# Hybrid decoder trunk on one core: unit norms on column and row tiles, and the delta scan's keys times state first

## Chip, cores and metric

One core of a Trainium2 chip runs the whole kernel. The metric is the time of one execution on the device in microseconds; 0.2% of it is 3.7 us.

## What is computed

Two layers of a decoder trunk, sequence 512, width 1024, all in f32. Each layer joins three token mixers (sparse attention A, gated delta rule B, retention C) by gates, projects, and adds a squared-ReLU MLP of width 4096. The change touches branch B, which has four heads of width 128:

```python
qb = l2_norm(qb.reshape(bsz, seq, B_HEADS, B_HEAD_DIM))   # x * rsqrt(sum(x*x) + EPS)
kb = l2_norm(kb.reshape(bsz, seq, B_HEADS, B_HEAD_DIM))
...
t_inv = solve_triangular(eye + m, eye)                    # m: strict lower part of k_beta @ k^T * decay
u = t_inv @ (v * beta);  w = t_inv @ (k_beta * exp(g))
# scan over chunks
v_new = u - w @ state
o = (q * exp(g)) @ state + a_intra @ v_new
state = state * exp(g_last) + (k * exp(g_last - g))^T @ v_new
```

## The kernel before

Weights stream from memory in slabs of 128x1024. GpSimd (or ScalarE) rounds a slab to a high part, VectorE subtracts to get the low part (L1094), and TensorE makes three products per tile (L1229 to L1231: high-high, high-low, low-high), 24 matmuls of 512 columns a slab. Raw, high and low parts have two buffers, so the low part of slab n + 2 is made after slab n has been used. Dense results go round four banks psD; the small matmuls go round three banks psM[0] to psM[2], with psM[3] for accumulations. small_bank (in the TensorE program) waits until the step that last had the bank has been read; `drained` names that reader, bank_plan (L612) gives the banks in TensorE's order.

The order is written in one list for all engines. Its prefix is by hand (L165 to L190): misc, twelve convolution slabs (keys, queries, values of the four heads) with SiLU, va, four rotation slabs, the first cv slab. `every` (L529) expands it: for each step its TensorE, ScalarE and VectorE part; a slab's low part for two slabs later (`lo`) comes on VectorE right behind the VectorE part of that slab's step. In the prefix the eight unit norms are spread over four rounds, two per round. One norm is unit_sq on ScalarE (squares to sqs, two buffers, L1764), a 128x128 matmul with ones (`unit`, L1362), which gives each of the 128 partitions the sum over the partitions, Ln and Exp on ScalarE into gt (L1772, L1774), and a product on VectorE (L2199). The first round is followed by `rows`, a transpose (L1395) of the decay columns.

The middle is planned by a list scheduler in the same file with a cost per step and a rank by the longest path behind it; it mixes the delta scan, retention, attention and slabs in four pieces. Each chunk n of 128 positions has four heads. In the scan vn, kk, kq and kn are turns and products of the chunk (L1294, L1288); then the 16x16 blocks are solved through memory and merged in levels (left, xx, xt; L1429, L1441, L1453). After them:

```python
# n >= 1, before
Kp = K[n] * (beta * exp(g))            # VectorE L2307, K[n] is kn's turned copy
wT = Kp^T X                            # TensorE L1288, ScalarE copies it times -1 to P1 (L1858)
v2 = X^T v + P1^T St                   # TensorE L1476, L1479, ScalarE copies (L1861)
oT = ...                               # TensorE L1489, L1492
St = St * exp(g_last) + K''^T v2       # VectorE L2324 (Sd), TensorE st L1288, VectorE L2331 (St)
```

where X is the inverse and K'' is K times kps (Kpp, L2319). A hand-written tail (the last gate and merge slabs, the output projection) and the MLP follow.

Of the kernel before, what the change touches and what calls it, by code (L numbers as in the profile page):

```python
# [23 lines left out]
ALU = mybir.AluOpType  # L24
# [3 lines left out]
P = 128  # L28
# [44 lines left out]
PIECES = 4  # L73

# [29 lines left out]
for _name, _w in (("ident", P), ("ones", P), ("cosA", S), ("sinA", S), ("cosI", S), ("sinI", S), ("cosR", S), ("sinR", S), ("decay", H * S),  # L104
                  ("tri", P), ("maskadd", P), ("cap", P),
                  ("level", (LEVELS - 1 - FIRST) * P)):
# [12 lines left out]
def tables():  # L119
# [32 lines left out]
    put("level", np.concatenate(lv, 1))  # L152
    return t
# [5 lines left out]
def schedule():  # L159
# [7 lines left out]
    for j in range(CONVS):  # L167
# [3 lines left out]
        if j >= 1:  # L171
            prefix.append(("silu", j - 1))
    prefix += [("va",), ("silu", CONVS - 1), ("unit_sq", 0), ("unit_sq", 1), ("decays",), ("rot", 0), ("va_turn",),
               ("gcum",)]
    for r in range(4):
# [4 lines left out]
        for j in (2 * r, 2 * r + 1):  # L180
            prefix.append(("unit", j))
            if j + 2 < 2 * H:
                prefix.append(("unit_sq", j + 2))
# [40 lines left out]
    for n in range(ST):  # L224
        for i, (x, t) in enumerate((("vn", .44), ("kk", .9), ("kq", .9), ("kn", .44))):
            drains = {"vn": ("dve", "vb", n), "kk": ("dve", "MT", n), "kq": ("dve", "AT", n), "kn": ("act", "K", n)}
            op("pe", x, n, t=t, to=drains[x], after=[("dve", "AT", n - 1)] + [("dve", "decay", n)] * (i > 0))
# [4 lines left out]
        op("act", "K", n, t=copied(), after=[("pe", "kn", n), ("act", "E", n)])  # L232
# [8 lines left out]
    for n in range(ST):  # L241
# [287 lines left out]
    def every(steps, n, ahead=()):  # L529
# [3 lines left out]
        for s in steps:  # L533
# [78 lines left out]
def bank_plan():  # L612
# [14 lines left out]
    for s in PE_ORDER:  # L627
# [7 lines left out]
        elif k in ("unit", "va_turn", "misc_turn", "fin", "gcum", "rows"):  # L635
# [52 lines left out]
def build(nc, ws, wo, wd, par, post, tab, x_in, out, rows_d, mt_d, x_d, xt_d):  # L688
    with ExitStack() as ctx:
# [45 lines left out]
        with ExitStack() as mix:  # L735
# [1981 lines left out]
```

## Time and profile before

| what | us |
|---|---|
| median of 3 runs (lowest, highest) | 1860.92 (1860.22, 1861.11) |
| the profiled execution | 1859.46 |
| its span, first to last instruction | 1857.6 |
| TensorE busy | 1830.2 |
| VectorE busy | 1247.8 |
| ScalarE busy | 750.9 |
| GpSimd busy | 265.4 |

The granted clock of TensorE was 0.998 of its full rate. Matmuls are pipelined: their busy times overlap, so the time that one occupies is read from the distance of two starts. An f32 matmul leaves two records; an fp32r matmul and an f32 transpose leave one. A layer takes about half of the span; the second layer's steps lie some 922 us after the first's.

### The profile page before, as it was taken

To read this page: it belongs to the slowest core of one execution; us is meant where nothing else is said; L and a number is where in the kernel's file an instruction comes from. 1 tells how busy PE (TensorE), PEld (TensorE's weight loads), DVE (VectorE), ACT (ScalarE), POOL (GpSimd) and SP (SyncE) were. 2 spreads that over 40 slices of the span, in tenths; PEclk is the share of its full clock that TensorE was granted. 3 is DMA by queue.
4 is the path that set the end of the run, shared out by engine and by line. 5 is a ranking of instruction groups with operands and counts; after the bars stand their busy time and mean duration, and the time that the engine had idled before them with its cause. 6 is when DMAs were issued, how large, how long until landed. Compare 5 with 4: busy or idle time off the path is not lost.

```text
span 1857.6 us, 23921 instructions
## 1 busy us (share of the span) xinstructions
PE 1830.2 (99%) x8878; PEld 1467.8 (79%) x8878; DVE 1247.8 (67%) x2072; ACT 750.9 (40%) x1261; POOL 265.4 (14%) x385
## 2 busy tenths in 40 slices
PE   8999999999999999999999999999999999999997
PEld 6877767788888888888778777677887888888886
DVE  6856789854475667575878658898534657575748
ACT  3163343322334635454531533533123346354454
POOL 2221111111120010000012211111112201100000
PEclk9999999999999999999999999999999999999999
DMA  6432113322441794766522322223225308856654
GB/s 239 146 126 85 62 63 98 88 80 69 145 150 46 210 255 138 202 181 170 166 100 93 125 74 69 69 89 97 80 69 190 138 13 249 226 150 191 194 135 102
DMA packets 87041, 240.22 MB, mean 129 GB/s; under 512 B 19920, under 2 KB 32400, under 8 KB 85904
## 3 DMA queue, kind: packets, MB, share of 16 engines
q1 hardware_dynamic: 46656, 171.76, 26.7%
q0 software_dynamic: 10368, 37.75, 10.9%
q10 hardware_dynamic: 29904, 29.19, 4.8%
q8 instruction: 72, 1.18, 0.3%
q14 instruction: 41, 0.34, 0.1%
HBM read 227.62 MB, written 11.06 MB: 128 GB/s over the span
## 4 chain that ended last, share of the span: by engine, by line
PE 90%; DVE 4%; ACT 3%; issue 2%; DMA 1%; DVEq 0%; POOL 0%; ACTq 0%; SPq 0%
PE psD L1229 24%; PE psD L1231 23%; PE psD L1230 23%; PE psM L1229 3%; PE psM L1230 3%; PE psM L1231 3%; PE psM L1288 1%; PE psM L1294 1%; PE psM L1507 1%; PE psM L1386 1%; PE psM L1525 1%; PE psM L1513 1%; PE psM L1378 1%; ACT wide L1757 1%; DVE wide L2536 1%
## 5 line engine op out<-in xcount | busy, mean ns | idle before, releaser
L1229 PE MATMUL psD<-a_hi,w_hi 128*128 128x512 f32 (+2 forms) x1488 | 595.3, 400 | 0.9 <-DVE w_lo L1094 0.6
L1231 PE MATMUL psD<-a_hi,w_lo 128*128 128x512 f32 (+2 forms) x1488 | 575.1, 386 | 0.0
L1230 PE MATMUL psD<-a_lo,w_hi 128*128 128x512 f32 (+2 forms) x1488 | 574.2, 386 | 0.0
L1094 DVE TENSOR_TENSOR w_lo<-raw,w_hi 128x1024 fp32r<-128x1024 f32 x216 | 263.5, 1221 | 142.6 <-POOL w_hi L1196 98.0
L1229 PEld LDWEIGHTS psD<-a_hi,w_hi 128*128 128x128 f32 (+1 forms) x1488 | 278.9, 187 | 79.3 <-issue 21.6
L1231 PEld LDWEIGHTS psD<-a_hi,w_lo 128*128 128x128 f32 (+1 forms) x1488 | 278.8, 187 | 57.8
L1230 PEld LDWEIGHTS psD<-a_lo,w_hi 128*128 128x128 f32 (+1 forms) x1488 | 279.2, 188 | 56.7 <-issue 4.8
L2524 DVE TENSOR_TENSOR d_lo<-d_raw,d_hi 128x1024 fp32r<-128x1024 f32 x102 | 124.1, 1222 | 69.2 <-ACT d_hi L2054 69.2
L1196 POOL TENSOR_SCALAR w_hi<-raw 128x1023 fp32r<-128x1023 f32 x150 | 166.2, 1108 | 0.0
L1195 POOL TENSOR_TENSOR w_hi<-raw,tabs 128x1 fp32r<-128x1 f32 x150 | 34.9, 233 | 896.3 <-PE psD L1231 865.3
L1203 POOL DMA_DIRECT2D d_raw<-in_wd x72 | 63.3, 961 | 642.8 <-DMA d_raw<-in_wd 437.7
L2054 ACT CAST d_hi<-d_raw 128x1024 fp32r<-128x1024 f32 x102 | 105.9, 1046 | 104.2 <-PE psM L1231 41.2
L2040 ACT CAST w_hi<-raw 128x1024 fp32r<-128x1024 f32 x62 | 65.1, 1049 | 84.8 <-PE psD L1231 84.3
L1229 PE MATMUL psM<-d_hi,f_hi 128*128 128x512 f32 x240 | 94.3, 393 | 0.1
L1230 PE MATMUL psM<-d_lo,f_hi 128*128 128x512 f32 x240 | 93.4, 389 | 0.0
L1231 PE MATMUL psM<-d_hi,f_lo 128*128 128x512 f32 x240 | 93.4, 389 | 0.0
L1757 ACT COPY wide<-psD 32x512 f32<-32x512 f32 (+1 forms) x84 | 48.7, 579 | 78.9 <-DVE iq L2184 34.5
L1229 PE MATMUL psD<-y_hi,w_hi 128*128 128x512 f32 x192 | 77.4, 403 | 0.0
L1231 PE MATMUL psD<-y_hi,w_lo 128*128 128x512 f32 x192 | 74.8, 390 | 0.0
L1230 PE MATMUL psD<-y_lo,w_hi 128*128 128x512 f32 x192 | 74.8, 390 | 0.0
L2048 ACT CAST f_hi<-gt 128x768 fp32r<-128x768 f32 x64 | 60.6, 947 | 29.3 <-DVE gt L2512 28.2
L2518 DVE TENSOR_TENSOR f_lo<-gt,f_hi 128x768 fp32r<-128x768 f32 x64 | 69.8, 1091 | 3.6
(301 smaller groups left out, 2786.5 us busy)
## 6 DMA issues: line engine op xcount, KB each, us to landing
raw<-in_ws SPq DMA_DIRECT2D x216, 512.0 KB, 3.5
d_raw<-in_wd SPq DMA_DIRECT2D x88, 512.0 KB, 5.9
d_raw<-in_wd POOLq DMA_DIRECT2D x72, 512.0 KB, 8.4
s_raw<-in_wo ACTq DMA_DIRECT2D x14, 512.0 KB, 11.5
tabs<-in_tab SPq DMA_DIRECT2D x2, 2880.0 KB, 12.0
x<-rows_d ACTq DMA_DIRECT2D x4, 1024.0 KB, 5.7
x<-out ACTq DMA_DIRECT2D x2, 2048.0 KB, 8.4
x<-in_x SPq DMA_DIRECT2D x4, 512.0 KB, 5.4
```

The costliest lines, as they stand in the source:

```text
L1094: dve.tensor_tensor(w_lo[:, s, :], raw[:, s, :], w_hi[:, s, :].bitcast(F32), ALU.subtract) \
L1196: pool.tensor_scalar(w_hi[:, s, 1:], raw[:, s, 1:], 1.0, 1.0, ALU.mult, ALU.mult) \
L1203: pool.dma_start(home(name), down_slab(c, b, j), accum_op=ALU.add).then_inc(*inc("sum_" + name[:None if name[0] == "C" else 1], 16))
L1229: pe.matmul(out, lhi, rhi, start=start, stop=False, skip_group_check=more)
L1230: pe.matmul(out, lhi, rlo, start=False, stop=False, skip_group_check=more)
L1231: return pe.matmul(out, llo, rhi, start=False, stop=stop, skip_group_check=more)
L1757: sig(act.copy(wt[to:to + n, 6 + r % 2, :], src[at:at + n, :]), "rot_copy" if to + n == P else "rot_part")
L2040: act.copy(w_hi[:, s, :], raw[:, s, :]).then_inc(sem("w_hi"), 1)
L2048: sig(act.copy(f_hi[:, p, w, :], fr[:, w, :]), "f_hi" + part)
L2054: sig(act.copy(operand(c, st)[0], source(st)), "d_hi")
L2518: sig(dve.tensor_tensor(f_lo[:, p, w, :], fr[:, w, :], f32(f_hi[:, p, w, :]), ALU.subtract), "f_lo" + part)
L2524: sig(dve.tensor_tensor(lo, source(st), f32(hi), ALU.subtract), "d_lo")
```

## The change

- The squares of four heads lie in one buffer, sq4, and each is made with the last four convolutions (keys) or behind the first sum (queries). sq4 lies where cv comes later.
- `usum` g makes four matmuls of 128 rows and 32 columns of ones, head h into partitions 32h to 32h + 31 of one bank. ScalarE takes Ln and Exp once for all four.
- `spread` g makes four matmuls of 32 rows with a table that is one in each first row of a quarter, each into a bank of its own (three of the small ones and psM[3]). VectorE multiplies straight with the banks.
- In the prefix: usum 0 ahead of rotation 0; spread 0, usum 1 and spread 1 behind rotations 1, 2 and 3.
- The scan multiplies keys by state first (`ks`), VectorE scales the product and subtracts it from v (`ku`, two products), and v2 is one matmul a head. Kp, wT and its copy go. The keys of chunk n are turned only behind ks; the last chunk's not at all.
- The table `first` adds 128 columns.

```diff
@@ -103,7 +104,7 @@
 _at = 0
 for _name, _w in (("ident", P), ("ones", P), ("cosA", S), ("sinA", S), ("cosI", S), ("sinI", S), ("cosR", S), ("sinR", S), ("decay", H * S),
                   ("tri", P), ("maskadd", P), ("cap", P),
-                  ("level", (LEVELS - 1 - FIRST) * P)):
+                  ("level", (LEVELS - 1 - FIRST) * P), ("first", P)):
     TAB[_name] = (_at, _w)
     _at += _w
 NTAB = _at
...
@@ -150,6 +151,7 @@
         a, b = row[:, None] >> l, row[None, :] >> l
         lv.append((b == a + 1) & (b % 2 == 1))
     put("level", np.concatenate(lv, 1))
+    put("first", np.repeat(row[:, None] % QUARTER == 0, P, 1))
     return t
 
 
...
@@ -170,17 +172,17 @@
             prefix.append(("misc_turn",))
         if j >= 1:
             prefix.append(("silu", j - 1))
-    prefix += [("va",), ("silu", CONVS - 1), ("unit_sq", 0), ("unit_sq", 1), ("decays",), ("rot", 0), ("va_turn",),
-               ("gcum",)]
+        if j >= CONVS - H:
+            prefix.append(("unit_sq", j - (CONVS - H)))
+    prefix += [("va",), ("silu", CONVS - 1), ("decays",), ("usum", 0)] + [("unit_sq", H + h) for h in range(H)]
+    prefix += [("rot", 0), ("va_turn",), ("gcum",)]
     for r in range(4):
         if r < 3:
             prefix.append(("rot", r + 1))
         else:
             prefix += [("piece", j, "cv", 0) for j in range(PIECES - 1)] + [("cv", 0)]
-        for j in (2 * r, 2 * r + 1):
-            prefix.append(("unit", j))
-            if j + 2 < 2 * H:
-                prefix.append(("unit_sq", j + 2))
+        if r < 3:
+            prefix.append((("spread", 0), ("usum", 1), ("spread", 1))[r])
         if r == 3:
             prefix.append(("rot", 4))
         prefix.append(("turn", r))
...
@@ -223,13 +225,16 @@
         op("dve", "decay", n, t=4 * read(1, slow), after=[("act", "decay", n)])
     for n in range(ST):
         for i, (x, t) in enumerate((("vn", .44), ("kk", .9), ("kq", .9), ("kn", .44))):
+            if x == "kn" and n:
+                continue
             drains = {"vn": ("dve", "vb", n), "kk": ("dve", "MT", n), "kq": ("dve", "AT", n), "kn": ("act", "K", n)}
             op("pe", x, n, t=t, to=drains[x], after=[("dve", "AT", n - 1)] + [("dve", "decay", n)] * (i > 0))
         op("act", "E", n, t=copied(), after=[("dve", "decay", n)])
         op("dve", "vb", n, t=read(4, 1.1), after=[("pe", "vn", n)])
         op("dve", "MT", n, t=read(4, slow) + read(), after=[("act", "E", n), ("pe", "kk", n), ("dve", "vb", n)])
         op("dve", "AT", n, t=read() + read(4, slow), after=[("pe", "kq", n), ("dve", "MT", n), ("act", "decay", n)])
-        op("act", "K", n, t=copied(), after=[("pe", "kn", n), ("act", "E", n)])
+        if n == 0:
+            op("act", "K", n, t=copied(), after=[("pe", "kn", n), ("act", "E", n)])
         if n + 2 < ST:
             op("act", "decay", n + 2, t=copied(), after=[("dve", "AT", n)])
             op("dve", "decay", n + 2, t=4 * read(1, slow), after=[("act", "decay", n + 2), ("dve", "decay", n + 1)])
...
@@ -260,16 +265,16 @@
             else:
                 op("pe", "xt", n, l, t=.55, to=("dve", "XT", n, l), after=[("act", "left", n, l), ("act", "XT", n, l - 1)])
                 op("dve", "XT", n, l, t=read(2, 1.2), after=[("pe", "xt", n, l)])
-        over = [("pe", "wT", n - 1)] if n >= 2 else []
         if n:
-            op("dve", "Kp", n, t=read(4, slow), after=[("act", "K", n), ("dve", "Kpp", n - 1)] + over)
+            op("pe", "ks", n, t=.9, to=("dve", "ku", n), after=[("dve", "St", n - 1), ("dve", "AT", ST - 1)])
+            op("dve", "ku", n, t=read(4, 1.1) + read(4, slow), after=[("pe", "ks", n), ("dve", "vb", n), ("dve", "Kpp", n - 1)])
+            if n < ST - 1:
+                op("pe", "kn", n, t=.44, to=("act", "K", n), after=[("pe", "ks", n)])
+                op("act", "K", n, t=copied(), after=[("pe", "kn", n)])
         if n < ST - 1:
-            op("dve", "Kpp", n, t=read(4, slow), after=[("act", "K", n), ("dve", "Kp", n), ("dve", "AT", ST - 1)])
-        if n:
-            op("pe", "wT", n, t=.9, to=("act", "wT", n), after=[("dve", "XT", n, LEVELS - 1), ("dve", "Kp", n)])
-            op("act", "wT", n, t=copied(), after=[("pe", "wT", n)])
-        op("pe", "v2", n, t=1.8 if n else .9, to=("act", "v2", n),
-           after=[("dve", "XT", n, LEVELS - 1), ("dve", "vb", n), ("act", "wT", n), ("dve", "St", n - 1)])
+            op("dve", "Kpp", n, t=read(4, slow), after=[("act", "K", n), ("dve", "AT", ST - 1)])
+        op("pe", "v2", n, t=.9, to=("act", "v2", n),
+           after=[("dve", "XT", n, LEVELS - 1), ("dve", "vb", n)] + [("dve", "ku", n)] * (n > 0))
         op("act", "v2", n, t=copied(), after=[("pe", "v2", n)])
         op("pe", "oT", n, t=1.8 if n else .9, to=("act", "oT", n), after=[("act", "v2", n), ("dve", "AT", n), ("dve", "St", n - 1)])
         op("act", "oT", n, t=copied(), after=[("pe", "oT", n)])
...
@@ -539,7 +544,7 @@
             if s[0] in STREAMED and s != ("rot", 4):
                 late.append(("dve", "lo", n + 2))
                 n += 1
-            if s[0] not in ("va", "silu", "unit_sq", "decays"):
+            if s[0] not in ("va", "silu", "unit_sq", "usum", "decays"):
                 o += late
                 late = []
         return o
...
@@ -632,7 +637,10 @@
                 [("p1" if k == "left" else "ro" if k == "rv" else k, *(s[1:2] if k == "rv" else s[1:]))]
             for name, b in zip(names, TAKEN[s]):
                 use(name, b)
-        elif k in ("unit", "va_turn", "misc_turn", "fin", "gcum", "rows"):
+        elif k == "spread":
+            for h in range(H):
+                use((*s, h), 3 if h == H - 1 else None)
+        elif k in ("usum", "va_turn", "misc_turn", "fin", "gcum", "rows"):
             use(s)
         elif k in ("rv", "av") and s[2] == 0:
             use(("ro" if k == "rv" else "ao", s[1]), 3)
...
@@ -747,6 +755,9 @@
                 cv = sb("cv", [P, ST, S], where=u)
                 rp = sb("rp", [P, 2, S], where=u)
             with ExitStack() as u:
+                sb("cqk_place", [P, 4, S], where=u)
+                sq4 = sb("sq4", [P, H, S], where=u)
+            with ExitStack() as u:
                 sc = sb("sc", [P, S], where=u)
                 work = sb("work", [P, S], where=u)
                 rl = sb("rl", [P, 2, S], where=u)
...
@@ -1035,8 +1051,8 @@
                 return [(f"X{a[0] % 2}", 2 * inner_count(*a))]
             if k == "xt":
                 return [(f"XT{a[0] % 2}", level_count(*a))]
-            if k == "wT":
-                return [("wTn", a[0])]
+            if k == "ks":
+                return [("Ku", 2 * a[0] - 1)]
             if k == "v2":
                 return [("vnew", a[0] + 1)]
             if k == "oT":
...
@@ -1354,12 +1370,20 @@
                         if r != 4:
                             dense_T(("rot", r))
 
-                    def unit(j):
-                        if j == 0:
-                            pe.wait_ge(kept["tables_in"], 16 * (layer + 1))
-                        pe.wait_ge(*on("unit_sq", j + 1))
-                        ps = small_bank(("unit", j))
-                        small_done(pe.matmul(ps[:, :], T("ones"), sqs[:, j % 2, :], start=True, stop=True))
+                    def usum(g):
+                        pe.wait_ge(*on("unit_sq", H * g + H))
+                        ps = small_bank(("usum", g))
+                        for h in range(H):
+                            ins = pe.matmul(ps[quad(h), :], T("ones")[:, 0:QUARTER], sq4[:, h, :], start=True, stop=True)
+                        small_done(ins)
+
+                    def spread(g):
+                        pe.wait_ge(kept["tables_in"], 16 * (layer + 1))
+                        pe.wait_ge(*on("unit_r", g + 1))
+                        spots = [small_bank(("spread", g, h)) for h in range(H)]
+                        for h in range(H):
+                            small_done(pe.matmul(spots[h][:, :], T("first")[quad(h), :], gt[quad(h), 2 + g, :],
+                                                 start=True, stop=True))
 
                     def cv_tiles(i, ts):
                         u = DENSE["cv", 0]
...
@@ -1459,26 +1483,17 @@
                                 pe.wait_ge(*on(s, v))
                             turn_heads(("xt", n, l), lambda h: B["X", n % 2][:, cut(h)])
 
-                    def scan_w(n):
-                        pe.wait_ge(*on(f"XT{n % 2}", level_count(n, LEVELS - 1)))
-                        pe.wait_ge(*on("Kp", n))
-                        by_heads(("wT", n), lambda h: B["Kp"][:, cut(h)], lambda h: B["XT", n % 2][:, cut(h)])
+                    def scan_k(n):
+                        pe.wait_ge(*on("St", n))
+                        by_heads(("ks", n), lambda h: kB(h, n), lambda h: B["St"][:, cut(h)])
 
                     def scan_v(n):
 
                         pe.wait_ge(*on(f"XT{n % 2}", level_count(n, LEVELS - 1)))
                         pe.wait_ge(*on("vb", n + 1))
                         if n:
-                            pe.wait_ge(*on("wTn", n))
-                            pe.wait_ge(*on("St", n))
-                        ps = small_bank(("v2", n))
-                        for h in range(H):
-                            ins = pe.matmul(ps[:, cut(h)], B["XT", n % 2][:, cut(h)], qkv[:, 2 * H + h, cut(n)],
-                                            start=True, stop=n == 0)
-                            if n:
-                                ins = pe.matmul(ps[:, cut(h)], B["P1", n % 2][:, cut(h)], B["St"][:, cut(h)],
-                                                start=False, stop=True)
-                        small_done(ins)
+                            pe.wait_ge(*on("Ku", 2 * n))
+                        by_heads(("v2", n), lambda h: B["XT", n % 2][:, cut(h)], lambda h: qkv[:, 2 * H + h, cut(n)])
 
                     def scan_o(n):
                         pe.wait_ge(*on("vnew", n + 1))
...
@@ -1758,21 +1773,18 @@
                                 "rot_copy" if to + n == P else "rot_part")
 
                     def unit_sq(j):
-                        if j >= 2:
-                            mid(act, ("unit", j - 2))
+                        if j >= H:
+                            mid(act, ("usum", 0))
                         act.wait_ge(*on("silu", j + 1))
-                        sig(act.activation(sqs[:, j % 2, :], qkv[:, j, :], ACT.Square), "unit_sq")
-
-                    def unit(j):
-                        ps = mid(act, ("unit", j))
-                        if j >= 2:
-                            act.wait_ge(*on("unit_done", j - 1))
-                        rt = gt[:, 2 + j % 2, :]
-
+                        sig(act.activation(sq4[:, j % H, :], qkv[:, j, :], ACT.Square), "unit_sq")
+
+                    def usum(g):
+                        ps = mid(act, ("usum", g))
+                        rt = gt[:, 2 + g, :]
                         sig(act.activation(rt, ps[:, :], ACT.Ln, bias=4 * EPS), "unit_ln")
                         own("unit_ln")
                         sig(act.activation(rt, rt, ACT.Exp, scale=-0.5,
-                                           bias=0.0 if j < H else float(-0.5 * np.log(P))), "unit_r")
+                                           bias=float(-0.5 * np.log(P)) if g else 0.0), "unit_r")
 
                     def cv_(i):
                         if i < 3:
...
@@ -1853,9 +1865,6 @@
 
                     def turned(n, l):
                         sig(act.copy(B["XT", n % 2], mid(act, ("xt", n, l))[:, :]), f"XT{n % 2}")
-
-                    def scan_w(n):
-                        sig(act.mul(B["P1", n % 2], mid(act, ("wT", n))[:, :], -1.0), "wTn")
 
                     def scan_v(n):
                         sig(act.copy(MT[n], mid(act, ("v2", n))[:, :]), "vnew")
...
@@ -2194,9 +2203,10 @@
                         own("rot_sin")
                         sig(dve.tensor_tensor(dst, dst, other, ALU.add), "rot_done")
 
-                    def unit(j):
-                        dve.wait_ge(*on("unit_r", j + 1))
-                        sig(dve.tensor_tensor(qkv[:, j, :], qkv[:, j, :], gt[:, 2 + j % 2, :], ALU.mult), "unit_done")
+                    def spread(g):
+                        for h in range(H):
+                            qk = qkv[:, H * g + h, :]
+                            sig(dve.tensor_tensor(qk, qk, mid(dve, ("spread", g, h))[:, :], ALU.mult), "unit_done")
 
                     def rp_(h, m):
                         i, w = RET[h, m], S - m * P
...
@@ -2298,14 +2308,16 @@
                         sig(dve.tensor_tensor(odd, odd, ps[0:HALF, 0:H * HALF].rearrange("p (h c) -> p h c", h=H),
                                               ALU.subtract), f"XT{i}")
 
-                    def kp_(n):
-                        if n == 1:
+                    def ku(n):
+                        v, t = qkv[:, 2 * H:, cut(n)], heads(B["Ku"])
+                        ps = mid(dve, ("ks", n))
+                        if n > 1:
+                            own("Ku")
+                        else:
                             own("bk")
-                        else:
-                            mid(dve, ("wT", n - 1))
-                        dve.wait_ge(*on("K", n + 1))
-                        sig(dve.tensor_tensor(heads(B["Kp"]), qkv[:, 0:H, cut(n)], over(egl[:, n * H:(n + 1) * H], P),
-                                              ALU.mult), "Kp")
+                        sig(dve.tensor_tensor(t, heads(ps[:, :]), over(egl[:, n * H:(n + 1) * H], P), ALU.mult), "Ku")
+                        own("Ku")
+                        sig(dve.tensor_tensor(v, v, t, ALU.subtract), "Ku")
 
                     def kpp(n):
                         k = qkv[:, 0:H, cut(n)]
...
@@ -2313,9 +2325,7 @@
                             dve.wait_ge(*on("esm", 3))
                             own("qs")
                             sig(dve.tensor_tensor(egl, beta, egc, ALU.mult), "bk")
-                            dve.wait_ge(*on("K", 1))
-                        else:
-                            own("Kp")
+                        dve.wait_ge(*on("K", n + 1))
                         sig(dve.tensor_tensor(k, k, over(kps[:, n * H:(n + 1) * H], P), ALU.mult), "Kpp")
 
                     def sd(n):
```

## Rows read from the trace of the kernel before

**Rows 1.** The page: busy time (share) xinstructions; chain that ended last, by engine.
```profile
PE 1830.2 (99%) x8878; PEld 1467.8 (79%) x8878; DVE 1247.8 (67%) x2072; ACT 750.9 (40%) x1261; POOL 265.4 (14%) x385
...
PE 90%; DVE 4%; ACT 3%; issue 2%; DMA 1%; DVEq 0%; POOL 0%; ACTq 0%; SPq 0%
```
**Rows 2.** Waits of TensorE by line: us in total, times, longest.
```profile
PE psM L1085 <- DVE wide L853: 11.1, 2, 7.6
...
PE psM L1362 <- ACT sqs L1764: 1.1, 2, 0.5
```
**Rows 3.** Timeline of TensorE around unit norms: start us, us, engine, line, operation.
```profile
106.84 0.39 PE L1231 MATMUL psD<-a_hi,w_lo 128*128 128x512 f32 x1
107.07 1.88 PE L1362 MATMUL psM<-sqs,tabs 128*128 128x512 f32 x4
108.79 0.27 PE L1395 MATMUL psM<-tabs,small 128*32 128x128 f32 x1
...
109.13 0.40 PE L1230 MATMUL psD<-a_lo,w_hi 128*128 128x512 f32 x1
...
128.60 0.39 PE L1231 MATMUL psD<-w_hi,a_lo 128*128 128x512 f32 x1
...
130.69 1.13 PE L1362 MATMUL psM<-sqs,tabs 128*128 128x512 f32 x2 [0.54 <-ACT sqs L1764]
...
131.89 0.39 PE L1230 MATMUL psD<-w_lo,a_hi 128*128 128x512 f32 x1
```
**Rows 4.** The same timeline behind the slab of va.
```profile
100.51 0.60 PE L1294 MATMUL psM<-tabs,bw 128*128 128x128 f32 x4
100.94 0.29 PE L1344 MATMUL psM<-small,tabs 128*128 128x16 f32 x2
101.55 0.47 PE L1229 MATMUL psD<-a_hi,w_hi 128*128 128x512 f32 x1 [0.31 <-DVE w_lo L1094]
```
**Rows 5.** The same timeline: a pair of 64-row matmuls; sixteen of 64x64.
```profile
168.29 0.39 PE L1231 MATMUL psD<-a_hi,w_lo 128*128 128x512 f32 x1
168.61 1.13 PE L1378 MATMUL psM<-cqk 64*128 64x512 f32 x4
169.67 0.50 PE L1229 MATMUL psD<-a_hi,w_hi 128*128 128x512 f32 x1
170.00 0.39 PE L1230 MATMUL psD<-a_lo,w_hi 128*128 128x512 f32 x1
...
408.54 0.68 PE L1429 MATMUL psM<-x 64*64 64x64 f32 x16
```
**Rows 6.** Timeline of VectorE, then of GpSimd, behind rotation 1.
```profile
107.27 0.69 DVE L2184 TENSOR_TENSOR cqk<-psD,tabs 128x512 f32<-128x512 f32 x1 [3.45 <-PE psD L1231]
108.56 1.23 DVE L1094 TENSOR_TENSOR w_lo<-raw,w_hi 128x1024 fp32r<-128x1024 f32 x1 [0.60 <-POOL w_hi L1196]
...
107.47 1.06 POOL L1196 TENSOR_SCALAR w_hi<-raw 128x1023 fp32r<-128x1023 f32 x1
```
**Rows 7.** Groups of VectorE by shape: busy, mean ns | idle before and its releaser.
```profile
L2199 DVE TENSOR_TENSOR qkv<-qkv,gt 128x512 f32<-128x512 f32 x16 | 11.1, 692 | 20.7 <-ACT gt L1774 20.7
...
L2184 DVE TENSOR_TENSOR cqk<-psD,tabs 128x512 f32<-128x512 f32 x8 | 5.5, 684 | 6.9 <-PE psD L1231 6.9
```
**Rows 8.** Timeline of TensorE: keys times keys between two slabs.
```profile
288.67 1.05 PE L1288 MATMUL psM<-qkv 128*128 128x128 f32 x8
...
289.80 0.40 PE L1230 MATMUL psD<-a_lo,w_hi 128*128 128x512 f32 x1
```
**Rows 9.** Groups of TensorE by shape: v2's second matmul, then the scan's wT.
```profile
L1479 PE MATMUL psM<-bw,x 128*128 128x128 f32 x48 | 9.3, 275 | 0.0
...
L1288 PE MATMUL psM<-x,bw 128*128 128x128 f32 x48 | 6.3, 275 | 0.0
```
**Rows 10.** The same groups from 431.8 to 472.9 us: the slabs there.
```profile
L1229 PE MATMUL psD<-a_hi,w_hi 128*128 128x512 f32 x18 | 7.8, 433 | 0.0
...
L1229 PE MATMUL psD<-y_hi,w_hi 128*128 128x512 f32 x8 | 3.5, 441 | 0.0
```

More of the change, by code:

```diff
@@ L73 @@
 PIECES = 4
+QUARTER = P // 4
 A11, A12, A22, S1, S2, S3, S4, A21 = range(8)
@@ L880, in build @@
         eg = [bw[:, 8 + i, :] for i in range(2)]
-        B = {"misc": bw[:, 8, :], "va": bw[:, 9, :], "rows": bw[0:2 * ST * H, 8, 0:P], "Kp": bw[:, 8, :], "St": bw[:, 9, :]}
+        B = {"misc": bw[:, 8, :], "va": bw[:, 9, :], "rows": bw[0:2 * ST * H, 8, 0:P], "Ku": bw[:, 8, :], "St": bw[:, 9, :]}
         gcr, br_ = [xw[:, n, :] for n in range(ST)], [xw[:, ST + n, :] for n in range(ST)]
@@ L976, in evens, with quad @@
             return ap.rearrange("p (m two b) -> p m two b", two=2, b=2 ** l)[:, :, 0, :]
+        def quad(h):
+            return slice(h * QUARTER, (h + 1) * QUARTER)
         def cut(n):
@@ L1011, in drained @@
                 return [("gc", 1)]
-            if k == "unit":
+            if k == "usum":
                 return [("unit_ln", a[0] + 1)]
+            if k == "spread":
+                return [("unit_done", H * a[0] + a[1] + 1)]
             if k == "misc_turn":
@@ L1554, in _ @@
                              "va": va_, "rot": rot,
-                             "unit": unit, "va_turn": va_turn, "cv": cv_, "rs": rs, "rv": rv, "rows": rows,
-                             "vn": vn, "kk": kk, "kq": kq, "kn": kn, "left": left, "xx": xx, "xt": xt, "wT": scan_w,
+                             "usum": usum, "spread": spread, "va_turn": va_turn, "cv": cv_, "rs": rs, "rv": rv, "rows": rows,
+                             "vn": vn, "kk": kk, "kq": kq, "kn": kn, "left": left, "xx": xx, "xt": xt, "ks": scan_k,
                              "v2": scan_v, "oT": scan_o, "st": st, "index": index, "as": as_,
@@ L1959, in _ @@
                     steps = {"norm": norm, "silu": silu, "decays": decays, "va": va_, "rot": rot,
-                             "unit_sq": unit_sq, "unit": unit, "misc": misc, "va_turn": va_turn, "cv": cv_, "ret": ret,
+                             "unit_sq": unit_sq, "usum": usum, "misc": misc, "va_turn": va_turn, "cv": cv_, "ret": ret,
                              "rows": rows, "rows_in": rows_in, "lasts": lasts, "decay": decay, "E": e_, "K": k_,
                              "mt_out": mt_out, "blk_in": blk_in, "y_out": y_out, "x_in": x_in_, "left": left, "XT": turned,
-                             "wT": scan_w, "v2": scan_v, "oT": scan_o,
+                             "v2": scan_v, "oT": scan_o,
                              "index": index, "sexp": sexp, "prob": prob, "pt": pt_, "attend": attend, "fin_sq": fin_sq, "fin": fin,
@@ L2446, in _ @@
                              "rot": rot, "turn": turn,
-                             "unit": unit, "rp": rp_, "lasts": lasts, "decay": decay, "vb": vb_, "MT": mt_, "AT": at_, "solve": solve,
-                             "lev": lev, "Kp": kp_, "Kpp": kpp, "lvl": lvl, "X": x_, "XT": xt_, "Sd": sd, "St": st_,
+                             "spread": spread, "rp": rp_, "lasts": lasts, "decay": decay, "vb": vb_, "MT": mt_, "AT": at_, "solve": solve,
+                             "lev": lev, "ku": ku, "Kpp": kpp, "lvl": lvl, "X": x_, "XT": xt_, "Sd": sd, "St": st_,
                              "lo": lambda n: lo_slab(dve, n), "index": index, "top": top, "smax": smax, "rinv": recip, "fin": fin,
```

## The prediction

> **What bounds the kernel now.** I read the page first. TensorE is busy 1830.2 of 1857.6 us and carries 90% of the chain that ended last [rows 1]: a change saves time only by what it takes out of TensorE's own row of work, and costs time where TensorE waits in order. Then its waits by line: 11.1 us at the starts of the layers, and 1.1 us before the unit norms; the scan's steps hardly appear [rows 2]. So I priced every TensorE step that is removed or added, and then looked for waits that other engines would now impose. The profiled execution took 1859.46 us, 1.86 more than its span and 1.46 less than the median of the runs; I sum against it and carry the difference over to the median.
>
> Busy times of TensorE overlap, so prices are differences of starts. The split matmul of the slabs has a pitch of 0.227 us (106.84 to 107.07 [rows 3]). The price of a step between slabs is from the last slab start plus 0.227 to the second slab start after it minus 0.227.
>
> **Unit norms, before.** Two norms (four records, as each f32 matmul leaves two) last from 107.07 to 108.79: 0.86 each. With the transpose of the rows behind them the stretch is 109.13 - 0.227 - 107.07 = 1.84, so that transpose costs 0.12. Three rounds of a layer cost 1.72 (one with the 0.12); the fourth goes from 128.60 + 0.227 to 131.89 - 0.227, 2.84, since it waits for squares (0.54 of it just before its second norm) [rows 3]. A layer: 3 x 1.72 + 0.12 + 2.84 = 8.12. Ahead of them, after va's turn (0.43) and gcum, the next slab waits 0.31 for its low part [rows 4].
>
> **Unit norms, after.** Two sums (four matmuls of 32 output partitions) and two spreads (four of 32 contracted partitions). The nearest row is the pair of 64-row matmuls of 512 columns at 168.61: the stretch is 170.00 - 0.227 - 168.29 - 0.227 = 1.26 where two full ones cost 1.72, and a gap of 0.09 precedes the group [rows 5]. So tiles run side by side and what is left is one matmul, 0.86, plus 0.40 of changing over. The 64x64 tiles (sixteen records in 0.68) use other rows and columns [rows 5]; no row has tiles that share their rows and differ in columns, as the sums have. Bounds for a group of four: 1.26 if all run together, 4 x 0.86 + 0.40 = 3.84 if one by one. I take 1.26, from the pair. The same section gives 2.38 times for three column tiles of 512 columns; no row here shows it.
>
> First sum: its squares are issued beside the last four convolutions and are ready when va's slab ends; 1.26. The second sum and the second spread find their inputs done a slab earlier (on ScalarE twelve of sixteen pairs of Ln and Exp go), 1.26 each.
>
> **The first spread brings a wait.** Behind it on TensorE stands the transpose of the rows. Small banks turn over three; after misc_turn, usum, va_turn, gcum and spread (0), the rows get the bank of the first factor of that spread, and must wait until VectorE has multiplied with it (unit_done 1). VectorE has, in its written order, first the rotation's product and the low part of the slab after next. Rotation 1 ends at T = 107.07 [rows 3]: the low part waits for GpSimd's high part (107.47 + 1.06) and runs 108.56 to 109.79, T + 2.7 [rows 6]. A product with a PSUM operand of 128x512 takes 0.68, one in SBUF 0.69 [rows 7]; so the first factor is used at T + 3.3 and TensorE, done with the spread near T + 1.1, stands until T + 3.4. With the transpose and the restart the stretch is 3.6, 2.2 of it new wait. Before, the rows waited only for ScalarE's Ln of an old norm. Behind the rows are queued rotation 2 and all slabs; there is no other TensorE work in the prefix to cover it. Bounds: no wait at all (1.38) if the product came ahead of the low part, 3.6 as written; the order is written, so 3.6.
>
> The decays move ahead of two squares on ScalarE, and an extra 1.26 lies before rotation 0; so the 0.31 wait [rows 4] goes. Layer after: 1.26 + 3.6 + 1.26 + 1.26 - 0.31 = 7.07 against 8.12: **-1.05**, for two layers -2.1.
>
> VectorE's sixteen products stay, with PSUM operands, at one price [rows 7]. The tables grow by 64 KB; no long wait of TensorE names them [rows 2], so nothing.
>
> **Scan, removed and added.** Four heads of 128x128 in eight records cost 289.80 - 0.227 - 288.67 = 0.90 with slabs on both sides and no gap [rows 8]. Per layer: wT three times, -2.70 (48 records in all [rows 9]); the second matmul of v2 three times, -2.70 (48 records); keys times state three times, +2.70; and the turn of the last chunk's keys, -0.43 (a turn has half the records [rows 4]). Sum **-3.1** a layer, -6.2. kn of chunks 1 and 2 only move. On VectorE Kp goes and ku brings two (0.69 each [rows 7]), three times a layer, +2.1; VectorE is not what ends the waits there. ScalarE loses three scalings and one copy.
>
> New chain per chunk: state, ks (0.90), two products of ku (1.38), two hand-offs (0.25 each, an estimate from 107.07 to the VectorE start at 107.27), then v2: 2.8 us. It lies beside slabs: from the first v2 to the end of the scan (431.85 to 473) 26 triples of slab matmuls are interspersed, 26 x 0.68 = 17.7 us [rows 10], against 3 x 2.8 = 8.4, and ks needs no inverse, so it can run while the blocks are inverted, where wT had to follow them. I set 0.25 a layer for steps that fall awkwardly: +0.5.
>
> **Sum.** -2.1 - 6.2 + 0.5 = -7.8: 1851.7 for the profiled execution, **1853.1** for the median.
>
> **Rivals.**
> (1) No wait before the rows. For it: the factor's product is short. Against: the order [rows 6]. Then -4.4 more: 1848.7.
> (2) The four column tiles of a sum don't run together, or only in part. For it: no row has such tiles. Against: pairs overlap fully. Whole: (3.84 - 1.26) x 4 = +10.3, 1863.4; in halves, 1858.3. This is also the case in which the change does not do what it says.
> (3) Slower: the scan's chain becomes the bound at the last chunk's v2. TensorE runs out of slabs between the scan's steps, and the saved matmuls turn into waits. Price: with every link uncovered 2 x 8.4 = 16.8 in place of the -6.2 + 0.5, so 1860.92 - 2.1 + 16.8 = 1875.6. It decides once more than 7.8 us stand uncovered and is slower by more than the measurement tells from 11.5 us. For it: chunk 3's steps end the planned part and behind them the order is fixed. Against: 17.7 us of slabs [rows 10], and the inverse, not the state, releases chunk 3 now.
>
> **How the numbers follow.** Forecast 0.57; rival 1 0.12; rival 2 whole 0.12, in part 0.09; rival 3 0.05; the rest, waits that I don't see, 0.05. About 0.2% (3.7 us) is what can be told from no change: faster means below 1857.2, slower above 1864.6. Faster: 0.57 + 0.12 + a third of the partial case + some of the rest, 0.74. Slower: rival 3 and part of the rest, 0.06. Same 0.20. The range leaves out rival 3 and the ends of the others: 1848.2 to 1862.8; the bottom is rival 1, the top near the whole of rival 2. The likeliest case alone spans 1851 to 1856.
>
> **What would show it.** Right: the sums and spreads as groups of eight records that last some 1.1 us each; one wait of about 2.2 us per layer before the transpose of the rows, released by VectorE's product; no wait for squares in the norms; 32 unit records gone, v2 of chunks 1 to 3 with eight records, and the slabs at the end of the scan still without gaps. Wrong: a sum that lasts over 2 us; waits of VectorE's ku before v2 that reach a microsecond; more idle time at the end of the scan than at present.

## The result, and the profile after

| what | us |
|---|---|
| before, median of 15 runs | 1860.92 (1858.08 to 1861.95) |
| changed, median of 15 runs | 1864.22 (1862.65 to 1866.51) |
| ratio, 95% interval | 1.002 (1.0013 to 1.0027) |
| profiled execution of the changed kernel | 1862.65, span 1860.6 |

The change is slower by 3.3 us where 7.8 us less were forecast; the range ended 1.4 us below it. The interval leaves out 1, though 3.3 us is less than the 3.7 that the prediction took for telling. The busy time of TensorE did fall (1830.2 to 1825.1 [rows 1]), so the work went and something else came. From the page of the changed kernel:

```profile
span 1860.6 us, 23827 instructions
...
PE 1825.1 (98%) x8854; PEld 1459.3 (78%) x8854; DVE 1250.2 (67%) x2078; ACT 733.7 (39%) x1229; POOL 261.6 (14%) x385
...
PE 92%; DVE 3%; ACT 2%; DMA 2%; issue 1%; POOL 0%; DVEq 0%; ACTq 0%; SPq 0%; POOLq 0%
```

The prefix went as it was priced. TensorE's timeline of the changed kernel, first sum, va's turn, the first spread with the rows' transpose, the second spread (answers to [rows 3] to [rows 5]):

```profile
94.19 1.06 PE L1377 MATMUL psM<-sq,tabs 128*32 128x512 f32 x8
...
100.77 0.60 PE L1310 MATMUL psM<-tabs,bw 128*128 128x128 f32 x4
101.20 0.29 PE L1360 MATMUL psM<-small,tabs 128*128 128x16 f32 x2
101.35 0.48 PE L1245 MATMUL psD<-a_hi,w_hi 128*128 128x512 f32 x1
...
106.69 0.39 PE L1247 MATMUL psD<-a_hi,w_lo 128*128 128x512 f32 x1
107.00 1.14 PE L1385 MATMUL psM<-gt,tabs 32*128 32x512 f32 x8
110.37 0.27 PE L1419 MATMUL psM<-tabs,small 128*32 128x128 f32 x1 [2.23 <-DVE qkv L2209]
110.50 0.47 PE L1245 MATMUL psD<-a_hi,w_hi 128*128 128x512 f32 x1
110.81 0.40 PE L1246 MATMUL psD<-a_lo,w_hi 128*128 128x512 f32 x1
...
122.82 1.14 PE L1385 MATMUL psM<-gt,tabs 32*128 32x512 f32 x8
```

Four column tiles (eight records) take 1.06, four row tiles 1.14: both kinds run side by side. The 0.31 wait behind va's turn is gone. The stretch of the first spread is 110.81 - 0.227 - 106.69 - 0.227 = 3.67 (3.6 forecast), 2.23 of it the wait for VectorE's first product. VectorE there, as the order said it would be (to [rows 6]):

```profile
107.11 0.69 DVE L2193 TENSOR_TENSOR cqk<-psD,tabs 128x512 f32<-128x512 f32 x1 [3.53 <-PE psD L1247]
108.41 1.23 DVE L1110 TENSOR_TENSOR w_lo<-raw,w_hi 128x1024 fp32r<-128x1024 f32 x1 [0.60 <-POOL w_hi L1212]
109.55 2.48 DVE L2209 TENSOR_TENSOR qkv<-qkv,psM 128x512 f32<-128x512 f32 x4
```

From the first transpose of misc to the first retention matmul the first layer takes 138.26 us in place of 139.33: 1.07 less, 1.05 forecast. In the second layer the same distance is 0.13 longer (139.52 in place of 139.39). What differs there is the clock: windows of the changed kernel, the first one of the gap told of below (columns: us; busy time and count of TensorE, its weight loads, VectorE, ScalarE, GpSimd; granted clock, DMA share, GB/s):

```profile
407.30:412.60 5.30, 2.20 (x42) 1.91 (x41) 5.13 (x8) 2.45 (x5) 1.21 (x2) 0.75 0.30 94
410.00:416.83 6.83, 5.41 (x26) 4.41 (x27) 3.20 (x7) 0.00 (x0) 0.00 (x0) 0.50 0.24 77
1034.60:1038.05 3.45, 3.45 (x10) 2.67 (x9) 2.48 (x4) 0.15 (x1) 0.00 (x0) 0.51 0.43 142
```

Right behind the second layer's wait of 2.23 us the granted clock is 0.51, the 1.2 GHz level, for 3.4 us. A longer such stretch lies at 410, and a third one, of 3.4 us, at the same place of the second layer (1338). The kernel before has only one between its start and its last microseconds, at 935, where the second layer starts and both kernels wait 3.51 us for VectorE; the changed kernel has that one too. The waits by line, to be held against [rows 2]:

```profile
PE psM L1101 <- DVE wide L864: 11.2, 2, 7.7
PE psM L1419 <- DVE qkv L2209: 4.5, 2, 2.2
PE psD L1245 <- issue: 4.3, 4, 1.8
PE psM L1465 <- ACT x L1863: 3.4, 2, 1.7
```

The second line was forecast. The last two were not: the fourth, and 3.2 of the 4.3 us of the third (1.40 and 1.82), lie behind the last mergeC slab; the rest of the third (0.84 at 907) stood in the kernel before too. The timeline of TensorE there, changed kernel:

```profile
407.03 0.39 PE L1247 MATMUL psD<-y_hi,w_lo 128*128 128x512 f32 x1
407.35 0.50 PE L1477 MATMUL psM<-x 64*64 64x64 f32 x5
...
407.81 0.51 PE L1453 MATMUL psM<-x 64*64 64x64 f32 x11
410.02 1.07 PE L1465 MATMUL psM<-x 64*64 64x32 f32 x16 [1.70 <-ACT x L1863]
412.49 0.77 PE L1245 MATMUL psD<-y_hi,w_hi 128*128 128x512 f32 x1 [1.40 <-issue]
```

and the kernel before:

```profile
405.05 0.68 PE L1425 MATMUL psM<-x,bw 64*64 64x64 f32 x8
405.65 1.16 PE L1489 MATMUL psM<-bw 128*128 128x128 f32 x8
406.65 1.06 PE L1288 MATMUL psM<-bw,qkv 128*128 128x128 f32 x8
407.93 0.65 PE L1453 MATMUL psM<-x 64*64 64x64 f32 x8 [0.22 <-ACT x L1851]
408.54 0.68 PE L1429 MATMUL psM<-x 64*64 64x64 f32 x16
409.83 0.66 PE L1441 MATMUL psM<-x 64*64 64x32 f32 x16 [0.61 <-ACT x L1851]
```

The first merge slab of branch A needs A's output split into high and low parts, which starts when the last mergeC slab is done (ScalarE casts of 2.18 us at 407.51, VectorE's differences of 2.49 us from 409.89 to 412.38). For some 5.5 us TensorE has no slab at all, only scan steps. Before there were six of them, with 4.47 us busy in 5.30 (row below); now three, with 2.20 us busy in 5.30 (first window above).

```profile
405.00:410.30 5.30, 4.47 (x65) 4.01 (x64) 5.13 (x8) 3.51 (x7) 1.22 (x2) 1.00 0.30 100
```

From the start of the last slab matmul ahead of it to the first behind it the gap lasts 5.46 us in both layers, and lasted 5.68 before. Two full steps of chunk 0, oT and st, were done earlier, at 367.9 and 368.9, where their 1.8 us displace slabs. The steps that are left wait for one another through ScalarE, whose copy for the last of them stands behind its four casts:

```profile
407.51 2.18 ACT L1931 CAST y_hi<-qa 128x512 fp32r<-128x512 f32 x4 [21.22 <-PE psD L1247]
409.60 0.37 ACT L1863 COPY x<-psM 128x256 f32<-128x256 f32 x1
```

From the first fin of branch C to the last of branch B the layers take 237.74 and 237.31 us in place of 235.50 each, where 3.1 less was forecast.

**Theory.** (1) The two waits that TensorE has now (before the rows' transpose, and in the gap) cost themselves. (2) The clock falls in or behind them and makes the slabs that follow slow. **Rivals.** The clock has no part; or the scan's longer chain is what holds TensorE; or the scan's part is worth nothing in any order.

### The profile page after: what moved, and what is told of

The parts are those of the page before. It is cut to its first block, busy times and chain, and to the rows that moved or that the text cites. A ratio compares the mean times of both kernels' runs of the same rounds, so it can differ in the third digit from the quotient of the medians.

```text
span 1860.6 us, 23827 instructions
## 1 busy us (share of the span) xinstructions
PE 1825.1 (98%) x8854; PEld 1459.3 (78%) x8854; DVE 1250.2 (67%) x2078; ACT 733.7 (39%) x1229; POOL 261.6 (14%) x385
## 4 chain that ended last, share of the span: by engine, by line
PE 92%; DVE 3%; ACT 2%; DMA 2%; issue 1%; POOL 0%; DVEq 0%; ACTq 0%; SPq 0%; POOLq 0%
PE psD L1245 24%; PE psD L1247 23%; PE psD L1246 23%; PE psM L1245 3%; PE psM L1247 3%; PE psM L1246 3%; PE psM L1304 2%; PE psM L1310 1%; DMA d_raw<-in_wd 1%; PE psM L1522 1%; PE psM L1410 1%; PE psM L1540 1%; PE psM L1528 1%; PE psM L1402 1%; PE psM L1546 1%
## 5 line engine op out<-in xcount | busy, mean ns | idle before, releaser
L1965 ACT ACTIVATE gt<-psD 128x512 f32<-128x512 f32 x32 | 19.1, 597 | 155.1 <-PE psD L1247 143.5
```

## The experiments

**norms_only and scan_only**: one part of the change each.

```diff
 # norms_only: unit_sq, usum, spread, first, sq4 and their order; scan as before
 # scan_only: ks, ku, kn behind ks, v2 with one matmul a head; norms as before
```

> The kernel before with the unit norms' part alone (sums on column tiles, spreads on row tiles, their order in the prefix); the scan is as before. Theory (two parts that each gain TensorE work, and waits behind which the clock falls): the prefix gains 1.1 us a layer as in the changed kernel's first layer, 2.1 in all, less 1.7 for each stretch of 3.4 us at half clock that follows the 2.2 us wait ahead of the transpose of the rows: 1858.8 to 1860.5. Rival (the groups of tiles themselves are dear): over 1862, with sums and spreads of over 2 us each. The scan's region shows the same steps and no half-clock stretch.

Measured: 1859.44 (1858.08 to 1861.8; ratio 0.9998, 0.999 to 1.0007). The region of the scan takes 235.52 and 235.50 us, as before; the waits before the rows stand (4.5 in all), and the clock is halved for 3.41 us at 1032, behind the second. Within the band; the interval does not tell this part from no change.

> The kernel before with the scan's part alone. Theory: 6.2 us of matmuls go, but behind the last mergeC slab, while ScalarE and VectorE split branch A's output, TensorE has only three scan steps left in place of six; so about 3.4 us of waiting in that gap per layer in place of 1.2 (+4.4 in all), and stretches at half clock behind it, 10 us of them in all as in the changed kernel (+5): 1862 to 1865. Rival (the new chain state, keys times state, two products, v2 is what ends late): waits of v2 on VectorE's ku of a microsecond each, and the gap as before. If neither holds: 1855.

Measured: 1864.32 (ratio 1.0021, 1.0012 to 1.0031). This part alone makes the whole loss. Its waits:

```profile
PE psD L1232 <- issue: 4.7, 4, 1.8
PE psM L1444 <- ACT x L1845: 3.4, 2, 1.7
```

Of the 4.7 us, 3.65 lie in the two gaps. Half-clock stretches at 414 (3.41 us) and 1339 (6.83 us), each in or behind a gap; the one at the second layer's start (936) is 6.83 here. No wait of v2 on ku is in the list, so the longer chain is not it.

**fill_rows and fill_hole**: nothing moves, TensorE gets idle work in front of a wait. The products are thrown away.

```diff
+spare = bank(DENSE[("rot", 2)])                      # fill_rows, ahead of the rows' wait
+for _ in range(2):
+    pe.matmul(spare[:, :], T("ones"), T("cosA"), start=True, stop=True)
 ps = small_bank(("rows",))
...
+ps = small_bank(("xx", n, l))
+if (n, l) == (2, 5):                                 # fill_hole, ahead of xx's wait
+    for _ in range(2):
+        pe.matmul(ps[:, :], T("ones"), T("cosA"), start=True, stop=True)
 pe.wait_ge(*on(f"P1{i}", level_count(n, l)))
...
+if step == ("merge", "A", 0) and j == 0:             # fill_hole, ahead of y_lo's wait
+    spare = bank(DENSE[step])
+    for _ in range(2):
+        pe.matmul(spare[:, :], T("ones"), T("cosA"), start=True, stop=True)
 pe.wait_ge(*on("y_lo", H * b + H))
```

> The changed kernel with two idle f32 matmuls of 128x512 (ones times a table, results overwritten) ahead of the wait before the transpose of the rows; they last 1.7 of the 2.2 us, and nothing else moves. Theory (the wait brings the clock down in the second layer): no half-clock stretch behind the first spread of either layer, the time falls by 1.7 us for each that goes: 1862 to 1863. Rival (the clock has no part in it, waits alone): the same time as the changed kernel or up to 0.4 more.

Measured: 1861.01 (1859.83 to 1862.24), 3.2 less than the changed kernel, 1 below the band, and no half-clock stretch behind either first spread:

```profile
1030.00:1040.00 10.00, 9.78 (x43) 6.30 (x42) 5.60 (x8) 2.56 (x5) 1.21 (x2) 1.00 0.28 99
```

In the profiled pair the second layer's prefix is 1.72 shorter (139.52 to 137.80), which is the price of one such stretch. The other 1.5 of the 3.2 us is put down to nothing here; the profiled executions lie only 1.1 apart (1862.65 and 1861.54).

> The changed kernel with two idle f32 matmuls ahead of the wait of the xx step behind the last mergeC slab and two ahead of the first merge slab of branch A; they cover most of the 3.1 us of waiting in that gap and move nothing else. Theory (clock falls behind the gap, 6.8 us at half clock in the first layer and 3.4 in the second): these stretches go and the time falls by up to 5.1 us: 1859 to 1861. Rival (waits alone): the same time or up to 0.8 more.

Measured: 1859.86 (1858.09 to 1862.87), 4.4 less. The clock in and behind both gaps is whole:

```profile
407.00:419.00 12.00, 12.00 (x79) 8.21 (x78) 5.73 (x10) 2.45 (x5) 1.21 (x2) 1.00 0.27 90
1332.00:1345.00 13.00, 13.00 (x84) 9.25 (x83) 7.92 (x14) 2.37 (x5) 2.35 (x4) 1.00 0.13 42
```

A stretch has come elsewhere, though: 3.41 us at 112, behind the first layer's wait for the rows, where the changed kernel had none, and 6.83 in place of 3.41 at the second layer's start (934); the one at 1034 is gone.

Useless work makes the kernel faster (ratios 1.0004, 0.9995 to 1.0013, and 0.9997, 0.9988 to 1.0006, against the changed kernel's 1.002, 1.0013 to 1.0027): the clock has its part. The scan's region is 235.70 here, 2.04 and 1.61 us shorter than in the changed kernel, with the same steps; that is what 6.83 and 3.41 us at half clock cost there. But 235.70 is not below the 235.50 of before: with a whole clock the scan's saving is still gone, so the other part of the loss is to be looked for in the gap, which held below bears out.

**rows_later**: the wait of the rows taken away by their order.

```diff
-if r < 3:
-    prefix.append((("rows",), ("rows_in",), ("lasts",))[r])
+if r:
+    prefix.append((("rows",), ("rows_in",), ("lasts",))[r - 1])
```

> The changed kernel with the transpose of the rows, their reading back and the last columns each one round later in the prefix, so that no step stands behind a bank that VectorE has yet to read. Theory: the two waits of 2.2 us go, and the half-clock stretch behind them: 1864.2 - 4.4 - 1.7 = 1858.1, down to 1856.5 if fill_rows's 3.2 us are what the clock gives back. Rival (the rows' way through memory is then late, and the decays or kk wait for it): 1862 or more, with new waits at the start of the scan.

Measured: 1857.03 (ratio 0.9982, 0.9973 to 0.999). The line of L1419 is gone from the waits and nothing late has come. The two prefixes are 2.22 and 3.99 us shorter than in the changed kernel; the stretch at 1034 is gone and that at 410 is 3.41 in place of 6.83.

**gate_later and gate_later_before**: a gate slab in the gap, with the changed and with the old scan.

```diff
-    for n in range(4):
-        slab("mgate", "A", n, to=[("act", "mgate", "A", n)], order=("mgate", "A", n - 1) if n else None,
...
+    def first_gates(ns, order):
+        for n in ns:
+            slab("mgate", "A", n, to=[("act", "mgate", "A", n)], order=("mgate", "A", n - 1) if n not in (0, 3) else order,
...
+    first_gates(range(3), None)
...
     split("A", [("pe", "mergeC", 3)])
+    first_gates([3], ("mergeC", 3))
```

> The changed kernel with one gate slab (mgate A 3) planned behind the last mergeC slab in place of ahead of it; the same work. Theory (the gap while branch A is split is what took the scan's gain): a slab of 5.4 us covers it, 3.1 us of waiting a layer and 10 us at half clock go: 1864.2 - 6.2 - 5.1 = 1852.9. Rival (the scan's longer chain holds TensorE wherever the slabs stand): waits come back behind, 1858 or more.

Measured: 1858.39 (ratio 0.9989), 5.5 above the value and inside the rival's band. The gap is full, and its half-clock stretches are gone, but taking a slab from ahead of mergeC lets other waits in there (at 370 to 381), that the changed kernel has not, 5.3 us in all:

```profile
PE psM L1457 <- ACT x L1871: 2.6, 2, 1.3
PE psM L1308 <- DVE x L2312: 1.5, 2, 0.8
PE psM L1481 <- ACT x L1867: 1.2, 2, 0.6
```

They stand before steps of the inversion (left, xt) and before chunk 0's v2, which waits for the inverse. So the scan's steps do hold TensorE, as the rival says, but not by the link that the change made longer: none of the waits is on ku.

> The kernel before with the same gate slab moved. Theory: its gap was nearly filled by six scan steps, 1.2 us of waiting a layer: 2.4 less, 1858.2; the scan's change, in this order of slabs, is then worth some 5 us. Rival (moving the slab is worth the same in both, so the scan's change brings nothing): 1850 to 1853.

Measured: 1867.96 (ratio 1.0036, 1.0024 to 1.0049): a miss by 10 us, and both theories were wrong on it. The old scan has a wait of 2.3 us per layer before the step xx, for ScalarE's copy of left ("PE psM L1445 <- ACT x L1855: 4.5, 2, 2.3") and half clock behind it at 377 (6.83 us) and 1306 (3.41 us). So this pair doesn't price the scan's part; the move empties one place to fill another.

> The changed kernel with both moves. Theory: both gains add, 1864.2 - 6.1 - 11.3 = 1846.8, with stretches at half clock only at the second layer's start and at the end. Rival (they overlap, since the clock falls elsewhere as in the first layer of fill_hole): 1850.

Measured: 1850.22 (ratio 0.9947, 0.9934 to 0.9959). That is the rival's figure, and a half-clock stretch of 3.41 us has come at 367. But the gains that gate_later and rows_later had by themselves, 5.8 and 7.2, add in full (1851.2); the 3.4 us that lack against the theory come from gate_later, which had itself stayed 5.5 above its value.

**held, held_rows, norms_rows**: the gap filled by the steps that had filled it. A rule in the scheduler; the work is unchanged, but the plan around the two steps moves as well (xx of the gap now comes behind it), so what is measured is the new order as a whole.

```diff
 if n[0] != "pe":
     return at
+if n in (("pe", "oT", 0),) and ("pe", "mergeC", 3) not in end:
+    return 1e9
```

> The changed kernel with one rule more in the plan: oT of chunk 0 (and so st behind it) is not issued before the last mergeC slab is done. The same work; the gap behind that slab then has seven scan steps in place of three. Theory (the gap has a fixed length, and the change left it empty): its waits fall from 3.1 us to under 1 a layer, the half-clock stretches behind it go, 1864.2 - 4.5 - 5 = 1854.7. Rival (the scan's chain then ends later and holds the last fin steps): 1859 or more, with waits before v2 or fin of a microsecond and more.

Measured: 1855.17 (ratio 0.9974, 0.9964 to 0.9984), 0.5 off. The timeline of TensorE in the gap:

```profile
403.92 1.05 PE L1506 MATMUL psM<-bw 128*128 128x128 f32 x8
404.81 1.06 PE L1306 MATMUL psM<-bw,qkv 128*128 128x128 f32 x8
405.70 0.60 PE L1312 MATMUL psM<-tabs,x 128*128 128x128 f32 x4
407.07 0.65 PE L1451 MATMUL psM<-x,bw 64*64 64x64 f32 x8 [0.77 <-ACT x L1869]
407.64 0.66 PE L1312 MATMUL psM<-tabs,x 128*128 128x128 f32 x4
408.32 0.65 PE L1479 MATMUL psM<-x 64*64 64x64 f32 x8
409.07 0.68 PE L1455 MATMUL psM<-x 64*64 64x64 f32 x16
```

Seven steps and one wait of 0.77, for a copy of ScalarE (at 406.34) that again stands behind the four casts; no half-clock stretch in or behind the gap (those behind the waits for the rows, at 111 and 1032, are there), and the scan's region takes 233.35 us in both layers: 2.15 less than before, 2.35 less than with the idle fill.

> The changed kernel with that rule and with the rows' steps one round later in the prefix, as in rows_later (1857.0). Theory: both waits are then out, 1857.0 - 9.5 = 1847.5, with half-clock stretches at the layers' start and the end alone. Rival: 1850 or more, as with the gate slab moved.

Measured: **1848.51** (1846.91 to 1849.02; ratio 0.9935, 0.9923 to 0.9948), the fastest of all, 12.1 below the kernel before (1860.61 in the same runs). One half-clock stretch is left besides the end, at 930.

> The norms' part alone, with the rows' steps one round later; the scan is that of the kernel before, with six steps in the gap. Theory: norms_only's 1859.4 less 4.4 of waiting and 1.7 of clock: 1853.3; the distance to held_rows is what the scan's part is worth when its gap is filled, the 6 us that were forecast. Rival (the scan's part is worth nothing in any order): within 2 us of held_rows.

Measured: 1852.68 (ratio 0.9958). Against held_rows the scan's part is worth 4.2 us, which is 2 x (235.48 - 233.35) = 4.3 by the regions.

## Why the prediction was wrong

- **Unit norms, after: right in each term.** Sums 1.20 where 1.26 was taken, spreads 1.27, the wait 2.23 (2.2), the 0.31 gone, the first layer's prefix -1.07 (-1.05). The row of the 64-row pair was a sound base for column tiles; rival 2 fell. So did the reading under which four tiles, their matmuls strictly in program order, would take 2.15: both kinds of groups are done in 1.06 to 1.14. The Trainium skill ("TensorE: Matmul & The Clock Gate", Packing small matmuls), on which that reading drew, gives a gain of 2.38 times for three column tiles; the runs show 4 x 0.86 / 1.20 = 2.9 times for four, which is of that size. The same section says that matmuls start and end in program order. The trace does not speak against that: the first records of the four tiles of a sum start 7 ns apart (94.185 to 94.205), the second ones 0.45 us later (94.638 to 94.658). What failed is the prediction's own step, that both records of one tile come before those of the next.
- **Scan, removed and added: right as work, wrong as time.** The step that failed is the one that laid the scan beside 17.7 us of slabs [rows 10] and took every removed matmul at its price. The prediction counted slabs from 431.85 on, behind the first v2 with two parts. The place that matters is 25 us earlier, where branch A is split and TensorE has no slab for some 5.5 us. The waits of the kernel before showed it, in two lines that [rows 2] leaves out and that come to more than the 1.1 us of the unit norms; the prediction passed over them and said that the scan's steps hardly appear:

```profile
PE psM L1441 <- ACT x L1851: 1.2, 2, 0.6
PE psM L1453 <- ACT x L1851: 0.4, 2, 0.2
```

Steps that lie in such a gap are free as long as they fit, and steps that are pulled out of it cost their full time elsewhere. The plan of the change pulled oT and st of chunk 0 out. Holding them back (held) brought most of what had been forecast: 4.3 of the 6.2 us less 0.5. The term of the sum that failed is thus -6.2 with its 0.5 for steps that fall awkwardly: -5.7 forecast, +3.4 measured when the scan's part stands alone (scan_only), -4.2 once the gap is filled. Some 1.4 of the forecast are left. The gap of held lasts 5.99 us against 5.68 before, which is 0.6 of it in two layers; its wait of 0.77 is no part of it, since the kernel before waited 0.83 in the same place. The other 0.8 stays open.

- **A term was missing: what a wait costs behind itself.** The sum had waits at their own length and put the clock behind them at nothing. fill_rows and fill_hole, which leave the schedule's order alone, give 3.2 and 4.4 us back; in their profiles one stretch (1.7) and the two of the gap (2.04 and 1.61) are the part that can be pointed at. From fill_hole to held, where the same gap is filled by steps that have to be done anyway, it is 4.7 more (1859.86 - 1855.17). The three add up to 12.3 us; forecast and result lie 11.1 apart. No run has all three at once, so this is an estimate from separate runs.
- **The rivals.** Rival 3 had the right kind of cause (TensorE out of slabs between scan steps) at the wrong place and with the wrong link: no run shows a wait of v2 on ku. Rival 1 was made true by rows_later and gave 7.2 us, 4.4 forecast; 6.83 us less at half clock go with the difference of 2.8.
- **What the runs don't settle.** Part of the median's 3.3 us lies outside the regions named: in the profiled pair 1.3 us less at the start and 1.1 us more between and behind the regions, both of the size by which executions of one kernel differ. Half of what fill_rows gave back has no place in its profile either.

## What to carry to other kernels

When the busiest engine is fed in order, price removed work by where it lies: look for the stretches in which that engine has no bulk work (here some 5.5 us while the next operand is prepared), list what fills them before and after, and keep enough there. A wait of two or three microseconds on TensorE is to be priced with what the granted clock does behind it (here stretches of 3.4 us at half clock, at 1.0 to 1.7 us each, behind 7 of 10 waits of 2.23 us), and a scheduler that models neither will move filler out of such a place without a sign. After a change of a step's cost, read the new order of the steps, not only the sum.

## What the runs showed of the hardware that I had not expected

- The granted clock falls to its lower level (1.2 GHz) behind waits shorter than the 3.5 us at the second layer's start: behind the 2.2 us wait of the rows in 7 of 10 cases (five profiled kernels, two layers), in or behind the gap with its 3.1 to 3.5 us of waiting in 8 of 8 (four kernels), and in none of the 16 and 12 cases where the wait or the gap was filled or absent, those of the kernel before among them. The 12 leave out the three kernels with a gate slab moved: there it fell at 367, or at 377 and 1306, by waits of 0.6 to 2.3 us of their own, and in gate_later not at all. A stretch lasts 3.41 or 6.83 us (those that the end of the kernel cuts off aside), whatever the wait. The same wait in the two layers of one kernel can end either way (changed kernel: not at 110, yes at 1034); no run shows what decides it, and as each kernel has one profile, none shows how much of the spread of the runs it makes.
- Two matmuls whose results nobody reads made the kernel 3.2 us faster (fill_rows), though the transpose behind them waits for the same product of VectorE.
- Products with PSUM operands of 128x512 took 0.681 us a piece on VectorE, no more than those in SBUF (0.692 [rows 7]).
